# Sparse attention on one Trainium2 core: rounded operand pairs in place of full-precision products, scaling in place, plain transposes

## The reference, cut to what matters

```
for each head h (group g = h // 8), query block b of 128 tokens:
    s_sel = q[b,h] @ k_selected[g, 0:128*(b+1)].T   + causal mask + mask of chosen 64-token blocks
    s_win = q[b,h] @ k_window[g, 0:128*(b+1)].T     + causal mask
    o[b,h] = gate_cmp * (p_cmp @ v_cmp[g])          # p_cmp, gated, comes from an earlier stage
           + gate_sel * softmax(s_sel) @ v_selected[g]
           + gate_win * softmax(s_win) @ v_window[g]
y = o @ w_nsa_out      # 1024 x 1024, the next stage
```

## Time and profile before

| | |
|---|---|
| median of 3 runs | 3397.25 us (3395.22 to 3398.74) |
| profiled execution, its own time | 3392.33 us |
| its span, first to last instruction | 3390.4 us |
| stage nsa_compressed | 2428.4 to 2472.4 us |
| TensorE busy | 3063.0 us, 90% |
| VectorE, ScalarE, GpSimd busy | 46%, 29%, 10% |
| granted TensorE clock, mean | 0.936 of 2.4 GHz |

### The profile page before, as it was taken

One profiled execution on the slowest core, in us unless ns is written; L12 is line 12 of the kernel. 1 busy time (PEld: TensorE's weight loads), 2 busy tenths in 40 slices (PEclk: granted clock), 3 DMA queues, 4 the chain that ended last, 5 costly groups with the idle time before them and its releaser, 6 DMA issues. The chain is left out here.

```text
span 3390.4 us, 35694 instructions
## 1 busy us (share of the span) xinstructions
PE 3063.0 (90%) x14655; PEld 2437.5 (72%) x14655; DVE 1548.5 (46%) x2074; ACT 978.2 (29%) x1354; POOL 328.7 (10%) x215
## 2 busy tenths in 40 slices
PE   3899999999989999999989899999679896699994
PEld 3777688888767778888768788777557674577773
DVE  3662255555365235545575465555454544211113
ACT  2233333223224333222233233442133322111111
POOL 0000003333000001333300000100100000000001
PEclk7999999999889999999989999999589998599997
DMA  3211124444221114433323224323220002299992
GB/s 103 70 55 38 50 87 130 132 131 130 69 63 50 38 56 130 135 113 116 121 62 91 84 94 94 110 95 126 78 125 1 1 32 95 88 352 369 366 356 106
DMA packets 280361, 384.83 MB, mean 114 GB/s; under 512 B 53636, under 2 KB 250500, under 8 KB 267140
## 3 DMA queue, kind: packets, MB, share of 16 engines
q1 hardware_dynamic: 269348, 344.74, 30.9%
q0 software_dynamic: 10752, 37.75, 2.9%
q10 hardware_dynamic: 96, 0.02, 0.0%
HBM read 340.50 MB, written 41.94 MB: 113 GB/s over the span
## 5 line engine op out<-in xcount | busy, mean ns | idle before, releaser
L195 PE MATMUL ps<-h_hi,w_hi 128*128 128x512 f32 x1760 | 712.5, 405 | 71.2 <-PEq L1267 23.6
L196 PE MATMUL ps<-h_lo,w_hi 128*128 128x512 f32 x1760 | 699.2, 397 | 0.0
L197 PE MATMUL ps<-h_hi,w_lo 128*128 128x512 f32 x1760 | 697.6, 396 | 0.0
L172 ACT ACTIVATE w_hi<-w_raw 128x2048 fp32r<-128x2048 f32 (+1 forms) x170 | 322.3, 1896 | 893.6 <-PE ps L197 885.4
L177 DVE TENSOR_TENSOR w_lo<-w_raw,w_hi 128x2048 fp32r<-128x2048 f32 (+1 forms) x170 | 438.2, 2578 | 220.6 <-ACT w_hi L172 220.6
L195 PEld LDWEIGHTS ps<-h_hi,w_hi 128*128 128x128 f32 x1760 | 336.8, 191 | 158.9 <-issue 83.1
L196 PEld LDWEIGHTS ps<-h_lo,w_hi 128*128 128x128 f32 x1760 | 337.0, 191 | 73.8 <-issue 3.6
L197 PEld LDWEIGHTS ps<-h_hi,w_lo 128*128 128x128 f32 x1760 | 336.0, 191 | 73.8
L196 PE MATMUL ps<-merged_lo,w_hi 128*128 128x512 f32 x640 | 255.3, 399 | 0.0
L195 PE MATMUL ps<-merged_hi,w_hi 128*128 128x512 f32 x640 | 252.2, 394 | 0.0
L197 PE MATMUL ps<-merged_hi,w_lo 128*128 128x512 f32 x640 | 250.9, 392 | 0.0
(11 more groups left out here) (422 smaller groups left out, 4351.2 us busy)
## 6 DMA issues: line engine op xcount, KB each, us to landing
w_raw<-in_w_in SPq DMA_DIRECT2D x284, 256.0 KB, 3.6
w_raw<-in_w_up SPq DMA_DIRECT2D x128, 256.0 KB, 3.5
w_raw<-in_w_down SPq DMA_DIRECT2D x128, 256.0 KB, 3.5
w_more<-in_w_exp_down SPq DMA_DIRECT2D x32, 1024.0 KB, 8.0
room<-in_w_ada SPq DMA_DIRECT2D x96, 256.0 KB, 6.1
w_raw<-in_w_exp_gate SPq DMA_DIRECT2D x16, 1024.0 KB, 9.4
w_raw<-in_w_exp_up SPq DMA_DIRECT2D x16, 1024.0 KB, 7.3
w_more<-in_w_exp_gate SPq DMA_DIRECT2D x16, 1024.0 KB, 9.3
```

What stands on the lines that cost most here:

```text
L172: act.activation(self.hi[:, q, :, 0:cols], raw[:, q, :, 0:cols], ACT.Copy).then_inc(self.hi_ready, 1)
L195: pe.matmul(out, w[0], x[0], start=start, stop=False)
L196: pe.matmul(out, w[0], x[1], start=False, stop=False)
L197: return pe.matmul(out, w[1], x[0], start=False, stop=stop)
```

## The change

- Scores: for b = 0 as before, but on the 64 rows of the head alone (so the zero-padded key copies go). For b above 0, queries and keys are split into fp32r pairs (`query_high`, `query_low`, `key_high`, `key_low`), and `products` makes each score bank of three fp32r matmuls.
- Scaling: no diagonal. VectorE scales the selected part of p in place (`tensor_scalar`), ScalarE the window part (`scale`, a copy with a scale).
- Turning: `pe.transpose`, one record each, back into the banks that held the scores.
- The turned blocks are evicted as a rounded pair: ScalarE `high` (both banks), VectorE `low` (both banks). They lie in `W.hi` and `W.lo`.
- Values: two heads at once, 256 columns; the weights are the value block's high and low parts side by side (128 columns), so that the two halves of the output partitions are two partial sums. `move` (ScalarE) and `add_halves` (VectorE) add them, twice per unit.
- Three bank pairs (n % 3) for scores and turned blocks; heads in the order 0, 2, 4, 6, 1, 3, 5, 7.
- `self.x` serves as room for p and the masks. It is written to DRAM in `nsa_compressed` and loaded again at the end of `nsa_attention`; `add_projection` waits for it.
- The splits of the first `w_nsa_out` tiles move from `nsa_project` to the end of `nsa_attention`, and the load of the second pair of tiles with them.

```diff
@@ nsa_project
-                self.issue2(sp, P_GA, P_NSAO)
+                self.issue2(sp, P_GA, P_NSAO - 1)
...
-                    W.split_hi(act, m + 1, q)
+                    if t < n:
+                        W.split_hi(act, m + 1, q)
...
-                    W.split_lo(dve, GA + t // 2 + 1, t % 2)
+                    if t < n:
+                        W.split_lo(dve, GA + t // 2 + 1, t % 2)
@@ nsa_attention, sync
+                sp.wait_ge(turned, N)
+                sp.dma_start(self.x[:].rearrange("p k s -> p (k s)"), self.kept_x(0)).then_inc(self.x_back, 16)
+                self.issue2(sp, P_NSAO - 1, P_NSAO)
@@ nsa_attention, tensor
                 def scores(n):
-                    if n >= 2:
-                        pe.wait_ge(maxed, 2 * n - 2)
+                    if n >= 3:
+                        pe.wait_ge(lo_taken, 2 * n - 4)
...
                 def turn(n):
-                    pe.wait_ge(p_ready, n + 1)
-                    if n >= 1:
-                        pe.wait_ge(t_taken, 2 * n)
+                    pe.wait_ge(sel_scaled, n + 1)
+                    pe.wait_ge(win_scaled, n + 1)
                     for ty in range(2):
                         for j in range(b + 1):
-                            mm = pe.matmul(t_ps(ty)[:, j * P:(j + 1) * P], p[:, n % 2, ty, j * P:(j + 1) * P], diag[:, n % 2, ty], start=True, stop=True)
+                            mm = pe.transpose(bank(n, ty)[:, j * P:(j + 1) * P], p[:, n % 3, ty, j * P:(j + 1) * P], self.c("ident"))
...
+                for n in range(N + 3):
+                    if n >= 3:
+                        values((n - 3) // 2, (n - 3) % 2)
+                    if n < N:
+                        turn(n)
+                    if n + 2 < N:
+                        scores(n + 2)
@@ nsa_attention, vector
+                def low(n):
+                    for ty in range(2):
+                        dve.wait_ge(hi_taken, 2 * n + ty + 1)
...
+                for n in range(N):
                     normalise(n)
+                    if n >= 1:
+                        low(n - 1)
+                    if n % per == 3 and n // per + 1 < len(units) and units[n // per + 1][1] > 0:
+                        query_low(n // per + 1)
+                    if n + 2 < N:
+                        softmax_max(n + 2)
+                    if n == 2 * per + 5:
+                        key_low(1)
+                    if n >= per and n % per in (0, 4):
+                        add_halves(n // per - 1, n % per // 4)
+                    if n >= per and n % per == 5:
+                        out_low(n // per - 1)
+                low(N - 1)
+                last = len(units) - 1
+                add_halves(last, 0)
+                W.split_lo(dve, NSAO, 0)
+                add_halves(last, 1)
+                out_low(last)
+                W.split_lo(dve, NSAO, 1)
@@ nsa_attention, scalar
+                def scale(n):
+                    act.wait_ge(gated, n + 1)
+                    act.activation(p[:, i, 1, 0:w], p[:, i, 1, 0:w], ACT.Copy, scale=inv[:, i, 1:2]).then_inc(win_scaled, 1)
...
+                act.activation(vv[:, :, :, 0], v_tokens, ACT.Copy).then_inc(v_hi, 1)
                 exps(0)
+                key_high(0)
+                for n in range(N):
+                    scale(n)
+                    if n >= 1:
+                        high(n - 1)
+                    if n + 1 < N:
                         exps(n + 1)
```

More of the change, by code:

```diff
@@ L2339, in _, with key_parts, head_of @@
+            def key_parts(part, g):
+                return o_parts[part][:, 4:6, :] if g == 0 else kk[part][:]
+            def head_of(n):
+                u, r = steps[n]
+                g, b = units[u]
+                return u, r, g, b, HPG * g + r, (b + 1) * P
             @block.sync
             def _(sp):
-                for i in range(5):
-                    part = self.d["slots"][(4 + i) * S:(5 + i) * S, :].rearrange("(p r) n -> p (r n)", p=P)
-                    sp.dma_start(part, self.x[:].rearrange("p k s -> p (k s)")).then_inc(filled, 16)
@@ L2348, in scores @@
                 def scores(n):
[L2349 to L2356 removed]
+                    u, r, g, b, h, w = head_of(n)
@@ new lines, in scores @@
+                    rows = slice(HD * (h % 2), HD * (h % 2) + HD)
+                    if n >= 3:
+                        pe.wait_ge(lo_taken, 2 * n - 4)
+                    if b > 0 and n % per == 0:
+                        pe.wait_ge(q_lo, u - g)
+                        pe.wait_ge(k_lo, g + 1)
+                    for ty in range(2):
+                        out = bank(n, ty)[:, 0:w]
+                        if b == 0:
+                            mm = pe.matmul(out, self.rp[rows, h // 2, 0:P], key_rows[rows, ty, g, 0:P], start=True, stop=True)
+                        else:
+                            q = [a[rows, u % 2, r // 2, :] for a in qq]
+                            mm = products(pe, out, q, [key_part(i, ty, g)[rows, 0:w] for i in range(2)], True, True)
@@ L2368, in turn @@
                     mm.then_inc(turned, 1)
[L2370 to L2383, removed]
@@ L2385, in _, with values @@
-                scores(0)
[L2386 to L2392, removed]
+                def values(G, half):
+                    u, r, g, b, h, w = head_of(2 * G)
+                    par, q0 = h % 2, r // 2
+                    out = self.ps[:, 6 + par, q0 * P:(q0 + 2) * P]
+                    if half == 0:
+                        pe.wait_ge(lo_taken, 4 * G + 4)
+                        if G == 0:
+                            pe.wait_ge(v_lo, 1)
+                        if G % 2 == 0 and u >= 1:
+                            pe.wait_ge(added, 2 * u - 1 + par)
+                    items = [(ty, j) for ty in range(2) for j in range(b + 1)]
+                    for ty, j in items[half * (b + 1):(half + 1) * (b + 1)]:
+                        v, end = vv[:, j, NG * ty + g].rearrange("p a e -> p (a e)"), (ty, j) == items[-1]
+                        for a in pt:
+                            if end and a is pt[1]:
+                                for i in range(2):
+                                    pe.matmul(out[HD * par:HD * par + HD, i * P:(i + 1) * P], self.vcmp[:, (h + 2 * i) % 4, g, :],
+                                              self.pct[:, (h + 2 * i) // 4, b * P:(b + 1) * P], start=False, stop=False)
+                            mm = pe.matmul(out, v, a[G % 2][:, ty, j].rearrange("p h s -> p (h s)"), start=(ty, j) == items[0] and a is pt[0],
+                                           stop=end and a is pt[1])
+                    if half == 1:
+                        mm.then_inc(valued, 1)
@@ new lines, in query_high, with key_high, move @@
+                def query_high(u):
+                    g, b = units[u]
+                    if u >= 2:
+                        act.wait_ge(s_ready, per * (u - 1))
+                    act.activation(qq[0][:, u % 2], self.rp[:, 4 * g:4 * g + 4, b * P:(b + 1) * P], ACT.Copy).then_inc(q_hi, 1)
+                def key_high(g):
+                    act.activation(key_parts(0, g), key_rows[:, :, g], ACT.Copy).then_inc(k_hi, 1)
+                def move(u, par):
+                    rows, others = slice(HD * par, HD * par + HD), slice(HD * (1 - par), HD * (1 - par) + HD)
+                    act.wait_ge(valued, 4 * u + 2 * par + 2)
+                    if u >= 1:
+                        act.wait_ge(o_lo, u)
+                    act.activation(other[rows], self.ps[others, 6 + par, :].rearrange("p (c t) -> p c t", c=4), ACT.Copy).then_inc(moved, 1)
@@ L2476, in _ @@
+                act.activation(vv[:, :, :, 0], v_tokens, ACT.Copy).then_inc(v_hi, 1)
                 exps(0)
[L2477 to L2483 removed]
+                key_high(0)
[4 more added lines that the diff above has]
+                    if n + 1 < N:
+                        exps(n + 1)
+                    if n % per == 2 and n // per + 1 < len(units) and units[n // per + 1][1] > 0:
+                        query_high(n // per + 1)
+                    if n == 2 * per + 3:
+                        key_high(1)
+                    if n >= per and n % per in (0, 4):
+                        move(n // per - 1, n % per // 4)
+                    if n >= per and n % per == 5:
+                        out_high(n // per - 1)
@@ L2485, in _ @@
+                high(N - 1)
+                last = len(units) - 1
+                move(last, 0)
+                act.wait_ge(valued, N // 2 - 1)
+                W.split_hi(act, NSAO, 0)
+                move(last, 1)
+                out_high(last)
+                W.split_hi(act, NSAO, 1)
             @block.gpsimd
```

173 lines of the change are left out of this document (88 added, 85 removed).

## The result

The changed kernel takes **3462.35 us** (3460.47 to 3464.62) against 3396.23 us for the one before on the same chip: 1.0194 times as long, interval 1.0177 to 1.0212. The forecast had the sign and the chain of waits, but it gave the low clock a third of its weight: 3432 was too low, and the time lies 2 us above the range. The profiled execution has a span of 3459.0 us, 68.6 more than before. One execution in experiment 3 (6709 us, clock 0.449) and one in experiment 6 (4581.9 us, clock 0.63) ran in a slow state and stay out of the ratios.

What follows compares the result with a forecast made beforehand. It took TensorE, busy 254 of 284 us in the attention stage, as the bound, and a closed chain of waits after the change. +20 us without the clock and +15 for it gave 3432 us, range 3408 to 3460.

Steps and rivals of the forecast that it cites:

- chain at 2.4 GHz: Attention stage: passes of 2.74, 3.71, 4.78 and 5.84 us at 128 to 512 keys; the steps gain nothing, +4 us.
- `add_halves`: Attention stage: two calls per unit in VectorE's order, 0.61 us each over 7 units, +8.5 us.
- tail: End of the attention stage: 13.7 us from the last turning to the next stage instead of 4.9, +8.8 us.
- start of `nsa_out`: After TensorE idles for 9 us in the tail, `nsa_out` begins at 1.2 GHz: +2.5 us (0 to 4).
- start, key and query splits: Attention stage: `exps(0)` stands behind the 1024-column copy of the values, +2 us; the splits hide in the wait for scores.
- clock: Attention stage: some passes run at 1.2 GHz, +17 us, less 2 us that the present start loses: +15 us.
- The closed chain: Attention stage: reciprocal, scale, `high`, `low`, scores and maxima wait in a circle each pass; the third bank pair doesn't open it.
- The price of a pass at 1.2 GHz: Attention stage: longer only by its scores, +0.46, +0.63, +0.94 and +1.24 us at 128 to 512 keys; +52 for all passes.
- I take a third of the passes: Attention stage: a third of the passes run at 1.2 GHz, +17 of the +52 us for the whole stage.
- The clock lifted once and kept: Rival, attention stage: the clock rises in the first or second unit and stays, 3417 us; chance 0.22.
- The clock at 1.2 GHz throughout: Rival, attention stage: transposes and gaps never lift the clock, +50 instead of +15, 3467 us; chance 0.10.
- The opened chain: Rival, attention stage: `scores(n+2)` runs beside `low(n-1)`, so VectorE doesn't stand still, -80 us, 3352 us; chance 0.10.

Runs made afterwards that it cites:

- experiment 3: The kernel before with VectorE scaling both parts of p in place and plain transposes, nothing else: 3371.15 us (0.9937).
- experiment 6: The changed kernel with two float32 filler products per pass on TensorE in the first 16 steps alone: 3462.15 us (1.0191).
- experiment 9: The changed kernel with filler in all steps, only ahead of the wait for the scaled p: 3435.86 us (1.0124).
- experiment 7: The changed kernel with both fillers in all steps, `move` and `add_halves` cut to 16 of 512 columns: 3423.67 us (1.0083).
- experiment 2: The changed kernel with three exchanges: `high(n-1)` before scaling n, `low(n-1)` before `normalise(n)`, `scores(n+2)` before `turn(n)`: 3402.26 us (1.0020).
- experiment 1: The changed kernel with two float32 filler products per pass on TensorE, ahead of and behind the wait for the scaled p: 3431.37 us (1.0101).
- experiment 5: The changed kernel with the three exchanged places, plus one float32 filler product per pass ahead of `scores(n+2)`: 3372.17 us (0.9930).
- experiment 10: The kernel before with one exchange alone, VectorE's `normalise(n)` ahead of the maximum of n+1: 3372.45 us (0.9934).
- experiment 4: The changed kernel with scores as one float32 product per bank instead of three fp32r products, at every width: 3498.13 us (1.0300).
- experiments 3 and 8: 8 is the kernel before with scaling in place, plain transposes and `normalise(n)` ahead of the maximum of n+1: 3336.63 us (0.9830).

## Why the prediction was right, and where it was wrong

The whole difference of 68.6 us, by stages and by the prediction's terms. The stages come from the first instruction of each in the two traces; the terms in the attention stage from the experiments. The line "what is left" is the remainder, so the column adds up to 68.6 by construction.

| term, us | predicted | measured | from |
|---|---|---|---|
| chain at 2.4 GHz | +4 | +5.4 | 16 x (17.15 - 16.81), experiment 9 |
| `add_halves` | +8.5 | +7.7 | experiment 7 |
| tail | +8.8 | +9.1 | 14.0 - 4.9 |
| start of `nsa_out` | +2.5 | +1.5 | rest of the span after the stage, 635.5 - 634.1 |
| `nsa_project` | -4.3 | -4.4 | 2384.69 - 2389.08 |
| `nsa_compress`, `nsa_compressed` | -1 | -2.9 | 2465.1 - 2472.4 at the start of the stage, plus 4.4 |
| start, key and query splits | +2 | about +5 | what is left; 2.2 of it is the start: 4.8 us to the first reciprocal, 2.6 before |
| sum without the clock | +20 | +21 | |
| clock | +15 | +47 | 0.80 of 16 x 3.83, below, less the 2 us that the old start lost |

- **The closed chain: shown.** At 2.4 GHz the passes are within 0.07 us of the computed ones at every width (experiment 9), and opening the chain takes 60 us off (experiment 2). That the third bank pair buys nothing, because `scores(n+2)` waits for `low(n-1)`, which is queued behind the scaling of the same pass, is read from the code and the waits; no run tried it alone.
- **The terms around it** hold to about a microsecond each, except that the two stages before gained 3 instead of 1 and that the remainder is 5 instead of 2. (The parts of the tail in the prediction add up to 13.3 us, not 13.7, which would have made it +8.4; and 0.9 of 3.4 us is a quarter of TensorE's work in transposes, not a third.) GpSimd's key copies beside VectorE and the weights' load beside the first DMA of `nsa_compress` are the likely two halves (0.7 and 2.2 us); neither was tried alone.
- **The price of a pass at 1.2 GHz: nearly right.** Measured, 3.23 - 2.7, 4.45 - 3.70, 6.0 - 4.85, 7.3 - 5.90: together 3.83 us, against 3.27 computed from the scores alone. The likely rest is the transposes, which at 1.2 GHz end later than `low` (by 0.3 us in the pass shown above).
- **The failed step is "I take a third of the passes".** 80% of the stage ran at 1.2 GHz: 0.80 x 16 x 3.83 = 49 us, where the term had 17. It is an estimate, and experiment 1 bears it out: 31 us less, although its filler costs 0.61 us over the four widths at 1.0, 10 us in all, and 3 us in the first three passes, together 44. I let passes of 384 and 512 keys keep a clock that had been lifted, from one stretch that was busy 2.40 of 4.0 us at 1.0. They lost it: in the changed kernel the clock was lifted in the second, third, fourth and eighth unit, eleven times, and fell again each time within 14 us. In experiment 6 TensorE was busy 1.30 of the 4.0 us before the fall, less than in my stretch. But before one of the falls in the third unit of the changed kernel it was 3.00, more than in my stretch, with 1.0 us of standing still at the end:

```profile
2563.10:2567.10 4.00, 3.00 (x17) 2.28 (x15) 1.94 (x7) 1.25 (x4) 0.00 (x0) 0.92 0.00 0
```

  So the busy share of one stretch elsewhere could not tell whether the clock would stay. What decides it is not settled by these runs.
- **That it is the clock and not something beside it: shown.** Filler work on TensorE, which can only delay, takes 31 us off (experiment 1) and 30 us off the opened chain (experiment 5); the same filler at the start alone takes nothing off (experiment 6).
- **The rivals.** The clock lifted once and kept (0.22): refuted by experiment 6. The clock at 1.2 GHz throughout (0.10, 3467): by its time the nearest, by mechanism not quite, since the clock is lifted in four of the eight units, with transposes among the work that lifts it. The opened chain (0.10): it is not what the kernel does. Opened by hand it is worth 60 us in experiment 2, and 59 between experiments 1 and 5, both with filler and a clock of 0.93 or more in the stage; I had computed 80.
- **What bounds the kernel before: wrong in part.** I took TensorE's 254 busy of 284 us as its bound. Experiment 10 takes 23 us off by exchanging two calls on VectorE, so TensorE's busy share hid a chain. That did not enter the sum, since the step lengths were read and not computed.

Of the change's parts, the plain transposes with the scaling in place (both parts on VectorE) are worth 26 us alone (3397.03 to 3371.15), and 36 on top of the better order (3372.45 to 3336.63). Of the rest only the fp32r scores were undone by themselves, and that made it slower (experiment 4); what the stacked values and the third bank pair do alone was not tried.

## What to carry to other kernels

When a change takes work from TensorE, compute the closed chain of waits first: if the pass doesn't shorten, the saved work turns into gaps, and in the gaps the clock can fall to half, which then slows the matmuls that are left on the chain. Read whether an engine is a bound from what waits for it and from an exchange of two calls, not from its busy share. A call's place in an engine's queue (here `normalise(n)` ahead of `softmax_max(n+1)`) can be worth as much as the arithmetic saved.

## What the runs showed of the hardware

- Extra matmuls made a kernel faster: 31 us less with two float32 filler products per pass, the granted clock of the stage going from 0.60 to 0.95.
- The clock fell after 4.0 us in which TensorE was busy 1.30 us (experiment 6), and elsewhere after 4.0 us in which it was busy 3.00 (the changed kernel, third unit); it rose there after 4.0 us without a pause at 0.5. The Trainium skill ("TensorE: Matmul & The Clock Gate", Part 1) describes such a gate, set by how busy TensorE has been recently; this trace agrees in kind.
- Transposes as a part of TensorE's work left the clock at 0.98 (experiments 3 and 8), as the transposes of the last stage had led to expect. The Trainium skill's rule that the full clock does not engage for transposes, quoted in the prediction, does not hold for this kernel.
